# Expert layer: token tiles 0 to 3 by dense matmuls over the streamed tables, tiles 4 to 7 by gather with diagonal weights, and attention ahead of both

## What is computed

```python
x = x + gate_m * (concat(rms_norm(y_ssm), rms_norm(y_attn)) @ w_out)
h2 = rms_norm(x, norm_ffn) * (1 + scale_f) + shift_f
q = (hc @ w_query).reshape(128, 8, 2, 128)              # hc: 128 tokens of h2, 8 heads
s = einsum('thpd,pkd->thpk', q, sub_keys)
s1, i1 = top_k(s[:, :, 0], 16); s2, i2 = top_k(s[:, :, 1], 16)
top_s, top_c = top_k(s1[..., :, None] + s2[..., None, :], 16)     # 16 of 256 sums
idx = e1 * 128 + e2                                     # e1, e2 looked up by top_c
a = gelu(einsum('thkd,td->thk', expert_down[idx], hc))
out = einsum('thk,thkd->td', softmax(top_s) * a, expert_up[idx])
```

## Time and profile before

| | us |
|---|---|
| median of 3 runs | 3248.66 (3248.62 to 3250.68) |
| span of the profiled execution | 3247.0 |
| phases ab, c, d | 0 to 399.7 |
| attention of tiles 0 and 1 | 399.7 to 427.1 |
| projections of tiles 0 and 1, first queries | 427.1 to 482 |
| slots, with the attention of tiles 2 to 7 between | 482 to 3247 |

### The profile page before, as it was taken

How to read it: one execution, slowest core, us unless ns; L and a number is a source line. 1 busy time by engine, 2 the same in 40 slices (tenths; PEclk the granted TensorE clock), 3 DMA queues, 4 the chain that set the end, 5 groups by cost and what they waited for, 6 DMA issues and landing times.

```text
span 3247.0 us, 38518 instructions
## 1 busy us (share of the span) xinstructions
PE 2362.8 (73%) x13186; PEld 1943.1 (60%) x13186; DVE 2206.0 (68%) x5266; ACT 2035.2 (63%) x3762; POOL 1321.2 (41%) x1190
## 2 busy tenths in 40 slices
PE   5977787777778797676676677766767667776766
PEld 4654456666666565565665566665666566665655
DVE  6881547767778576677666666666666666666654
ACT  3313416767777566676666766676667766766665
POOL 1140313323434344444445454444444444544543
PEclk9988998988878798777767776777677777767766
DMA  6600039988888999999999999999999999999997
GB/s 250 189 14 4 34 146 419 386 320 322 345 335 346 418 419 420 420 421 421 421 422 420 418 421 419 419 411 420 421 419 413 419 417 418 415 417 419 418 420 326
DMA packets 175461, 1162.57 MB, mean 358 GB/s; under 512 B 22720, under 2 KB 23632, under 8 KB 43808
## 3 DMA queue, kind: packets, MB, share of 16 engines
q0 software_dynamic: 148352, 1077.61, 81.0%
q1 hardware_dynamic: 25680, 78.30, 6.5%
q10 hardware_dynamic: 1232, 4.20, 0.3%
HBM read 1147.32 MB, written 11.53 MB: 357 GB/s over the span
## 4 chain that ended last, share of the span: by engine, by line
DMA 33%; DVE 23%; PE 16%; ACT 11%; issue 4%; POOL 1%; POOLq 0%; DVEq 0%; SPq 0%
DMA pair<-in_experts_dram,idx_g 32%; DVE pair L1693 11%; PE acc_a L1357 5%; ACT pair L1492 5%; PE pef L1332 3%; PE acc_b L1357 2%; ACT L1488 2%; PE acc_b L1237 1%; ACT w L1490 1%; PE pef L1256 1%; ACT pex L1433 1%; DVE top_i L1621 1%; DVE staged L1622 1%; ACT ga L1488 1%; DVE top_i L1624 1%
## 5 line engine op out<-in xcount | busy, mean ns | idle before, releaser
L1192 POOL DMA_INDIRECT pair<-in_experts_dram,idx_g x1024 | 1215.8, 1187 | 1484.1 <-PE acc_a L1357 865.1
L1693 DVE SCALAR_TENSOR_TENSOR pair<-pair,h 128x1024 f32<-128x1024 f32 x1024 | 1247.3, 1221 | 666.2 <-DMA pair<-in_experts_dram,idx_g 664.7
L1357 PE MATMUL acc_a<-ident,pair 128*128 128x128 f32 x5120 | 878.7, 333 | 443.2 <-ACT pair L1492 435.4
L1492 ACT ACTIVATE pair<-pair,w 128x1024 f32<-128x1024 f32 x1024 | 1176.2, 1149 | 33.3
L1357 PEld LDWEIGHTS acc_a<-ident,pair 128*128 128x128 f32 x5120 | 738.1, 173 | 576.3 <-ACT pair L1492 546.0
L1357 PE MATMUL acc_b<-ident,pair 128*128 128x128 f32 x3072 | 592.6, 361 | 292.9 <-ACT pair L1492 292.4
L1357 PEld LDWEIGHTS acc_b<-ident,pair 128*128 128x128 f32 x3072 | 488.6, 187 | 391.4 <-ACT pair L1492 386.7
L1488 ACT ACTIVATE ga<-a 128x1 f32<-128x1 f32 x1024 | 204.1, 199 | 687.3 <-DVE pair L1693 682.5
L1490 ACT ACTIVATE w<-ga,g 128x1 f32<-128x1 f32 x1024 | 301.6, 295 | 33.2
L1332 PE MATMUL pef<-h2t,wq 128*128 128x128 f32 x1536 | 196.6, 291 | 1.6 <-DMA wq<-in_w_query_t_dram 1.6
L1332 PEld LDWEIGHTS pef<-h2t,wq 128*128 128x128 f32 x1536 | 195.0, 209 | 2.8 <-issue 2.8
(11 more groups left out here) (341 smaller groups left out, 2365.6 us busy)
## 6 DMA issues: line engine op xcount, KB each, us to landing
wada<-in_w_ada_t_dram SPq DMA_DIRECT2D x48, 512.0 KB, 5.8
pair<-in_experts_dram,idx_g POOLq DMA_INDIRECT x1024, 16.2
pieces<-in_w_query_t_dram SPq DMA_DIRECT2D x16, 512.0 KB, 8.2
wq<-in_w_query_t_dram SPq DMA_DIRECT2D x4, 2048.0 KB, 35.9
ht<-in_x_t_dram ACTq DMA_DIRECT2D x4, 1024.0 KB, 15.1
wout_a<-in_w_out_dram SPq DMA_DIRECT2D x1, 4096.0 KB, 13.1
x2s<-out_dram SPq DMA_DIRECT2D x8, 512.0 KB, 12.3
out_dram<-h SPq DMA_DIRECT2D x8, 512.0 KB, 8.9
```

What stands on the lines that cost most here:

```text
L1192: p.indirect_dma_start(pair[n % R], None, A["experts"], bass.IndirectOffsetOnAxis(ap=idx[:, t % (2 * PH), k:k + 1], axis=0)).then_inc(pair ...
L1357: last = t.matmul(accs[ACC[i]][:, k * P:(k + 1) * P], pair[n % R][:, D + k * P:D + (k + 1) * P], S.ident[:], is_transpose=True, start=n % ...
L1492: s_.activation(pair[n % R][:, D:], pair[n % R][:, D:], ACT.Copy, scale=w[:, n % NA:n % NA + 1]).then_inc(scaled, 1)
L1693: v.scalar_tensor_tensor(down, down, 1.0, h2[:, n // P, :], ALU.mult, ALU.mult, accum_out=a[:, n % NA:n % NA + 1]).then_inc(dotted, 1)
```

## The change

- Token tiles 0 to 3 no longer gather. For them the kernel runs over all 16384 experts in 128 steps of 128 experts. `hidden(s)` multiplies a transposed tile of the down table (`d_ring`, 512 KB, from the new input `down_t`) by the h2 of the 512 tokens: 8 matmuls of 512 columns. ACT applies gelu (`activated`), DVE multiplies by a 128 x 512 tile of gates (`gate_hidden`, `g_ring`, 256 KB). After 4 such steps (a chunk), 8 `sums(u)` of 4 matmuls of 512 columns each multiply by 4 tiles of the up table (`u_ring`, 512 KB each), and DVE adds them in SBUF (`add_sums`).
- The gates are a table in DRAM of 16384 x 512 floats with padded rows (34 MB). SP fills it with zeros by 65 DMAs of 512 KB in phase c. DVE finds the choices of tiles 0 to 3 as before ("F" tasks), and POOL scatters each (head, rank) of a tile by one indirect DMA with add: 128 elements of 4 bytes. There are 4 x 8 x 16 = 512 of them, 64 ahead of the first gather and 448 in the list of the slots.
- Tiles 4 to 7 ("G" tasks) gather in 512 slots, R = 7. ACT no longer scales the up half, but makes a diagonal matrix (`diag`) of the weights from the identity, and `add_up` is 2 matmuls of 512 columns of the diagonal and the up half.
- Attention and projection of all 8 tiles stand ahead of the slots, and so do the first 10 of 32 query steps; a query step is now 8 matmuls of 512 columns for four tiles at once. In attention the copy out of PSUM (`at_turned`) goes from DVE to ACT.

The steps of the dense work are spread evenly over slots N0 = 172 to 505 by `WORK`; `SCATTER` puts 4 scatters in each of 112 slots between 33 and 176, in seven runs of 16. The core of the diff:

```diff
+NF = 4
+PITCH = P * NF * P + 1024
...
+            for j in range(S.gates_parts):
+                sp.dma_start(gates[:, j * D:(j + 1) * D], zeros[:]).then_inc(S.gates_zero, 16)
...
+            if w_at + 10 > at:
+                at, room = w_at + 10, 0
+            for f in range(NF * b, NF * b + NF):
+                for k in range(TOPK):
+                    SCATTER.setdefault(at, []).append((f, k))
+                    room += 1
+                    if room == 4:
+                        at, room = at + 1, 0
...
+    N0 = max(SCATTER) - 4
...
+    steps = [("S", s) for s in range(CHUNK)]
+    for c in range(NB // CHUNK):
+        more = [("S", s) for s in range(CHUNK * (c + 1), min(CHUNK * (c + 2), NB))]
+        steps += more[:1] + [("U", u) for u in range(8 * c, 8 * c + 8)] + more[1:]
+    WORK, spent = {}, 0.0
+    per_slot = (2.0 * NB + 8 * NB // CHUNK) / (SLOTS - 6 - N0)
+    for step in steps:
+        WORK.setdefault(N0 + int(spent / per_slot), []).append(step)
+        spent += 2.0 if step[0] == "S" else 1.0
...
+            def down_tile(b):
+                if b >= 4:
+                    sp.wait_ge(hid_done, b - 3)
+                sp.dma_start(d_ring[:, b % 4].rearrange("p k n -> p (k n)"), A["down_t"][b]).then_inc(down_gate_in[b % 4], 16)
...
+                    sp.wait_ge(hid_mul, b - 3)
+                sp.dma_start(g_ring[:, b % 4], gates[:, b * NF * P:(b + 1) * NF * P]).then_inc(down_gate_in[b % 4], 16)
...
+                    sp.wait_ge(sum_done, 8 * ((b - 4) // CHUNK + 1))
+                sp.dma_start(u_ring[:, b % 4], up[b]).then_inc(u_in[b // CHUNK % 2], 16)
...
+            for c in range(NB // CHUNK - 1):
+                b = CHUNK * (c + 1)
+                down_tile(b)
+                gate_tile(b)
+                for m in range(4):
+                    up_tile(b + m)
+                for m in range(1, 4):
+                    down_tile(b + m)
+                    gate_tile(b + m)
...
+                    if i == 0:
+                        hold(pool, gates_ready, h + 1)
+                    if h >= 1:
+                        hold(pool, put[i], 16 * TOPK * h)
+                p.indirect_dma_start(S.gates, bass.IndirectOffsetOnAxis(ap=idx_f[:, f % 16, k:k + 1], axis=0),
+                                     g_f[:, f % 16, k:k + 1], None, compute_op=ALU.add).then_inc(put[i], 16)
...
             def add_up(n):
...
-                pe.wait_ge(scaled, n + 1)
+                    pe.wait_ge(acc_read, n // P)
+                pe.wait_ge(diag_ready, n + 1)
+                for m in range(2):
+                    last = t.matmul(pa[:, m * 512:(m + 1) * 512], diag[:, n % ND, :], pair[n % R][:, D + m * 512:D + (m + 1) * 512],
...
+            def hidden(s):
+                if s == 0:
+                    pe.wait_ge(s_out, len(QSTEPS))
+                if s >= 2:
+                    pe.wait_ge(hid_out, s - 1)
+                pe.wait_ge(down_gate_in[s % 4], 32 * (s // 4 + 1))
...
-                    last = t.matmul(accs[ACC[i]][:, k * P:(k + 1) * P], pair[n % R][:, D + k * P:D + (k + 1) * P], S.ident[:],
-                                    is_transpose=True, start=n % P == 0 and k % 4 == 0, stop=n % P == P - 1,
-                                    skip_group_check=True)
...
+                    last = t.matmul(s_banks[s % 2][:].rearrange("p (m n) -> p m n", n=P), d_ring[:, s % 4, k, :],
+                                    h2t_f[:, :, k * P:(k + 1) * P], start=k == 0, stop=k == KD - 1)
+                last.then_inc(hid_done, 1)
...
+                if u % 8 == 0:
+                    pe.wait_ge(hid_mul, CHUNK * (c + 1))
+                    pe.wait_ge(u_in[c % 2], 16 * CHUNK * (c // 2 + 1))
+                if u >= 4:
+                    pe.wait_ge(sum_out, u - 3)
+                for r in range(CHUNK):
+                    b = CHUNK * c + r
+                    last = t.matmul(u_banks[u % 4], w_ring[:, b % 6, i * P:(i + 1) * P], u_ring[:, r, m * 512:(m + 1) * 512],
+                                    start=r == 0, stop=r == CHUNK - 1)
+                last.then_inc(sum_done, 1)
...
+            for s in range(4, POST_Q):
+                queries(s)
+                scores(s)
+            for n in range(TOTAL):
...
+                for kind, s in WORK.get(n, ()):
+                    if kind == "S":
+                        hidden(s)
+                    else:
+                        sums(s)
+                if 1 <= n <= SLOTS:
+                    add_up(n - 1)
...
-                s_.activation(pair[n % R][:, D:], pair[n % R][:, D:], ACT.Copy, scale=w[:, n % NA:n % NA + 1]).then_inc(scaled, 1)
...
+                if n >= ND:
+                    act.wait_ge(up_used, n + 1 - ND)
+                s_.activation(diag[:, n % ND, :], S.ident[:], ACT.Copy, scale=w[:, n % NA:n % NA + 1]).then_inc(diag_ready, 1)
...
+            def add_sums(u):
+                to = acc_f[:, (u % 8) // 2, (u % 2) * 512:(u % 2) * 512 + 512]
+                dve.wait_ge(sum_done, u + 1)
+                if u < 8:
+                    v.tensor_copy(to, u_banks[u % 4]).then_inc(sum_out, 1)
+                else:
+                    dve.wait_ge(sum_out, u - 7)
+                    v.tensor_tensor(to, u_banks[u % 4], to, ALU.add).then_inc(sum_out, 1)
```

More of the change, by code:

```diff
@@ new lines, in phase_ef @@
+    TASKS = [("F", f) for f in range(4)] + [("G", 0)]
+    left = list(range(4, 8 * NF))
+    for t in range(1, 8 * NG):
+        TASKS.append(("G", t))
+        TASKS += [("F", f) for f in left[:3]]
+        left = left[3:]
+    ORDER = {task: n for n, task in enumerate(TASKS)}
+    FRONT_PARTS = {}
+    for n in range(4 * PARTS):
+        FRONT_PARTS.setdefault(54 + n // 2, []).append((TASKS[n // PARTS], n % PARTS))
+    SLOT_PARTS, WEIGHED, BATCHES = {}, {}, [("F", 0), ("G", 0)]
+    stream = [(task, m) for task in TASKS[5:] for m in range(PARTS)]
@@ new lines, in phase_ef @@
+    n, taken = 0, 0
+    for task, m in stream:
+        if task[0] == "G" and m == 0 and n < 16 * (task[1] - 1):
+            n, taken = 16 * (task[1] - 1), 0
+        SLOT_PARTS.setdefault(n, []).append((task, m))
+        taken += 1
+        if m == PARTS - 1 and (task[0] == "G" or task[1] % NF == NF - 1):
+            at = n
+            while at in WEIGHED:
+                at += 1
+            WEIGHED[at] = len(BATCHES)
+            BATCHES.append((task[0], task[1] if task[0] == "G" else task[1] // NF))
+        if taken == 1 + n % 2:
+            n, taken = n + 1, 0
@@ L1037, in phase_ef @@
+    TOTAL = max(SLOTS + 2, max(WORK) + 2)
+    END = {P * (j + 1) + 1: j for j in range(NG)}
     with ExitStack() as ctx:
@@ L1150, in _ @@
+            for i in range(NF):
+                sp.wait_ge(fin_ready, NG + i + 1)
+                sp.dma_start(out[i], acc_f[:, i]).then_inc(stored_f, 16)
+            sp.wait_ge(stored_f, 16 * NF)
+            sp.wait_ge(stored, 16 * NG)
         @block.gpsimd
@@ L1343, in scores @@
+            def scores(s):
+                q, n = QSTEPS[s]
+                pe.wait_ge(q_out, s + 1)
+                for m in range(4):
+                    last = t.matmul(qs[:, m * PK:(m + 1) * PK], qt_sb[:, m * P:(m + 1) * P], skt[:, n, :], start=True, stop=True)
                 last.then_inc(s_done, 1)
             def add_up(n):
-                i = n // P
                 if n == 0:
-                    pe.wait_ge(a_out, FIRST)
-                elif n % P == 0 and i < 3:
-                    pe.wait_ge(acc_read, i)
-                elif n == 3 * P:
-                    pe.wait_ge(a_out, NT)
-                elif n % P == 0:
-                    pe.wait_ge(acc_read, i - 1)
@@ L1422, in _ @@
[L1422 removed]
+                if m in (4, 7):
+                    row(1 if m == 4 else 2)
+                for i in range(NT):
+                    if m == base(i) + 2:
+                        project_ssm(i)
+                    if m == base(i) + 3:
+                        at_back(i)
+                    if m == base(i) + 5:
+                        project_att(i)
+                    if m == TURN_AT[i]:
+                        turn(i)
+                if m in FRONT_Q:
+                    queries(FRONT_Q[m])
@@ L1754, in _ @@
+            weigh(1)
+            for n in range(TOTAL):
+                for kind, s in WORK.get(n - 1, ()):
+                    if kind == "S":
+                        gate_hidden(s)
+                    else:
+                        add_sums(s)
+                if n < SLOTS:
+                    dot(n)
+                for task, k in SLOT_PARTS.get(n, ()):
+                    find_part(task, k)
                 if n in WEIGHED:
-                    own.wait()
                     weigh_less(WEIGHED[n])
```

905 lines of the change are left out of this document (423 added, 482 removed).

## The result

The changed kernel takes 5049.7 us (median of 4 runs, 5043.8 to 5060.77) against 3248.64 us: a ratio of 1.556, 95% interval 1.553 to 1.558. The forecast was 4756, its range 4340 to 5400; the measured time is 294 us over it.

A forecast was written before the change was run, and what follows sets the result against it. The prediction took DMA transfers, 2.5 us a slot, to bound the kernel before. Its terms, 399.7 + 410 + 57 + 88 + 112 + 922 + 2748 + 18 + 1.7, summed to 4756 us; range 4340 to 5400.

The forecast's parts named there:

- the part that was kept for dearer scatters: Rival: scatters land one by one or hold DMA engines, 5647 us, chance 0.14; the range included 2.5 us a scatter.
- A: Phases ab, c, d at the start: 399.7 us, with the new zero fill adding 0.
- B and C: Ahead of the slots: attention and projections of all tiles, 410 us, and six more query steps, 57 us.
- D: 64 scatters ahead of the first gather: 88 us, at 1.24 us each plus 8 for the first landing.
- E: Slots 7 to 32: 26 slots at 4.3 us, 112 us, with DVE and PE waiting for each other at times.
- F: Slots 33 to 176: 922 us, POOL issuing 448 scatters and 144 gathers in order at 1.49 us each.
- G: From about slot 170 to the end: 2748 us, PE's passes 2346, chunk stalls 366, small terms 15 and 20.
- H: The end: 18 us for last copies, gates and stores, and 1.7 us outside the span.
- The bound of 3.2 us: Upper bound for a scatter, landing one by one like a 16 KB transfer: +766 us in F, +125 in D.
- rival 2: No stall at the chunks of the dense work, down tiles come in time: 4390 us, chance 0.13.
- rival 3: PE's clock stays low in the dense stage, 0.72, making 2346 us 3258: 5668 us in all, chance 0.07.
- rivals 4 and 5: PE passes cheaper: under 0.25 us with transfers the bound, faster than before, 0.03; or by two fifths, 3818 us, 0.03.

The follow-up runs named there:

- the last experiment: On the changed kernel with SP's tile order already changed, the turning of the keys waits for the keys alone, not also w_out's 4 MB: 4578.8 us, ratio 1.410.
- the kernel without stalls: The changed kernel with SP issuing a chunk's three down and gate tiles ahead of its four up tiles: 4584.1 us, ratio 1.411.

## Where the prediction was right, and where not

The direction, the mechanism and the order of the stretches came out as told. The time did not: 5049.7 us lies over the forecast's own 4550 to 5000, and inside the wider range only by the part that was kept for dearer scatters. Scatters were dearer, at 1.85 us and not at the 2.5 of that part; they gave more than half of the 294 us, and the stalls and the front the rest. By its own steps:

| step | forecast | measured | off by |
|---|---|---|---|
| A, with the zero fill | 399.7 | 400.6 | +1 |
| B and C, front | 467 | 490.6 | +24 |
| D, 64 scatters, and E | 200 | 244.7 | +45 |
| F, slots 33 to 176 | 922 | 1062.3 | +140 |
| G, dense work | 2748 | 2832.8 | +85 |
| H, with what lies outside the span | 19.7 | 18.7 | -1 |

- **A** was right: phase d ended 0.9 us later than before. The fill went at the upper rate of the forecast: its 65 DMAs were issued from 201.3 to 281.4 us, at about 405 GB/s, ahead of phase d's weights.
- **B and C** missed 24 us of 490. As a sum it was good enough; whether its straight line of items from tiles 0 and 1 to tile 7 holds was not looked at by itself. One piece not seen is the 11.9 us for w_out, but by the last experiment it can't simply be counted among them.
- **D, E and F** fell by one term, mis-sized: the price of a scatter. The forecast took the gather's issue and gap, 1.24 us in D and 1.49 in F; it is 1.55 + 0.30 = 1.85, because of the add. In D, 64 x 0.61 = 39 of the +45; the other 6 were not followed. In F, 448 x 1.85 + 144 x 1.3 = 1016 in place of 882: +134 of the +140. The sentence that failed is "both kinds write a list of 128 rows, so I take the gather's row": a sound guess on the list, and blind to the operation. The bound of 3.2 us held it; the price lies a fifth of the way from 1.49 to it.
- **G** was right in its large part: 2346 us of passes were forecast, 2354.04 stand in the kernel without stalls. The stall was the mis-sized term: 11.8 us a chunk forecast, (388 + 77) / 31 = 15.0 measured, 99 us more in all; the small terms came out 13 us under the 35 forecast. The landing was under-sized, 12.5 against 10: SP's five issues ahead of the gate tile's take some 3 us of it by themselves (2280.79 to 2283.70), and three more pairs of tiles are issued close behind. The clock was under-sized too, 2.5 against 1.8.
- **The Trainium skill.** Its sum for one DMA ("DMA: Bandwidth & Descriptors", anatomy of one DMA) gives 8.6 us for the 2.75 MB, an estimate: the section is on one DMA issued from GpSimd, and here six of SP's follow one another. From the first up tile's issue to PE's start were 12.6, so it errs further than the row of w_out did. Its spacing of 131 ns for a stream of matmuls of 512 columns ("TensorE: Matmul & The Clock Gate", back-to-back issue gap) is not what this kernel sees: 2354.04 us for 5460 recorded passes at a granted clock of 1.00 are 0.43 us a pass. These matmuls are float32, in two recorded passes each; no run here shows another type.
- **The rivals.** Scatters were dearer, though not by landing: POOL's issues bind, and the landings overlap. That they hold the DMA engines was true in part: these were 0.23 busy in D with next to nothing moved, but only 0.59 in F. The stall was there, against rival 2. The clock in G was 0.92 and 1.00 without the stalls, against rival 3; the low clock of before went with PE's idle time (582 of 1930 us). Passes were no cheaper, against rivals 4 and 5.
- **What would be needed to win** was told too mildly, though the number was there: of the 1280 us of transfers that 512 slots take, the kernel without dense work keeps 141. Attention in front (some 400 us) and the scatters (677) had spent nearly all of them before the first dense matmul. No run puts attention back between the slots, so what its place costs in the changed kernel is a difference of stretches and not an experiment.

No version here that computes everything beats the kernel before. The best is SP's new order, 4584.1 us or, within its spread, with the keys early, 4578.8: both 41% slower.

## What to carry to other kernels

To trade a bound on transfers for work of an engine, sum that engine's passes first, and then time the kernel with the new work left out: what remains must already be far below the old time. In a list that streams tables, issue what the waiting engine needs next ahead of what it needs later; here the place of one loop of two lines cost 466 us. And an operation inside a transfer, such as the add of a scatter, has a price of its own on the engine that issues it.
